# Retention value rows through DRAM and a broadcast DMA instead of broadcast products, on one core

## Chip, cores and metric

One Trainium2 chip, one core. The metric is the device time of one launch in microseconds (us); the kernel before takes 787.32 us, the median of 3 runs (786.14 to 787.53).

## The reference, cut to what matters

One layer of a hybrid decoder runs over 16 learned meta tokens, 256 prompt tokens and 8 samples of one token each, all in float32: RMSNorm, a mixer (gated convolution and retention), then a mixture of 16 experts. For the samples the retention carries a recurrent state of 4 heads x 256 x 512 per sample, which is read, changed and written back:

```
proj = h @ w_in          # glu_a, glu_b, q, k, v, g_ret, gate_a, gate_b
# per sample b and head h (one token, L = 1):
S_new[b,h] = gamma_h * S[b,h] + outer(k[b,h], v[b,h])   # 256 x 512
o[b,h]     = q[b,h] @ S_new[b,h]                        # 512
# prompt: the same with a decay mask over the tokens
x = x + W_o(sigmoid(gA) * Conv(h) + sigmoid(gB) * Retention(h))
x = x + HierMoE(RMSNorm(x))
```

32 states (8 samples x 4 heads) of 512 KB each go in and 32 come out.

## The kernel before, in words

The mixer is a list of 112 units (`UNITS`), each one block of 128 output features: 24 products over 8 blocks of depth in three parts (high times high, high times low, low times high). Units 0 to 15 are the convolution's gate, 16 to 31 q and k, 32 to 47 v, 48 to 63 g_ret, 64 to 79 the retention's output, 80 to 95 the gates, 96 to 103 the convolution's output, 104 to 111 w_o. All engines walk the same list in program order. For each unit ACT rounds a weight piece to its high part two units ahead (`hi`, L761), VectorE subtracts it for the low part (`lo`, L1101), TensorE multiplies (`passes`, L1602), and ACT or VectorE takes the result out of PSUM. SP loads weights, a chunk of 1 MB for two units, into 3 slots (`load_weights`, L594); its queue is in order.

For a v unit TensorE transposes the values back to tokens (L1700) and ACT copies them to `v_tok` (L891, L892); rows 16 to 23 of the third token tile belong to the samples. ACT and VectorE split those rows into a high and a low part in `v_two` (L963, L1265).

From unit `STEP0` = 37 on, each unit carries one of 22 retention steps k; `ON_AT`, which sets in which unit ACT and VectorE round the retention's parts, follows from it. Step k < 16 serves head k // 4 and two samples. What happens to a state n = 2k + j:

- POOL loads it into slot n % `SLOTS` (L654). There are 7 slots: four in `S_ring`, one in `S_five`, two in the idle `xT` (`S_more`).
- ACT multiplies it by gamma (`scaled`, L788): the odd one at the head of unit k, the even one at the end of the unit before.
- TensorE lays the sample's value row over all 128 partitions in a PSUM tile `vb` by a product of a one-column selector (`pick`, broadcast to 128 columns; made by ACT, L811 to L814) with `v_two` (L1762).
- VectorE adds k times that row to the state, in two halves (L1284), and frees the PSUM tile.
- POOL stores the state (L661) once VectorE has updated it; TensorE multiplies q with it one step later (`samp_o`, L1660), which counts `S_used`.

POOL's queue is written out by hand and in order: store(n), then wait that store(n - 1) has landed and that TensorE has used state n - 1, then load(n - 1 + SLOTS). Steps with k % 4 == 0 also make the prompt's new state (L1713, copied by ACT, L905, stored by POOL, L672), scores (L1723) and transposes (L1731); k % 4 == 1 the prompt's outputs (L1747). Later steps take means and variances (L1776, L1783) and, in 20 and 21, turn the last convolution rows. PSUM tiles go round 7 banks in one fixed order (`TILES`).

The convolution is 248 steps on VectorE (L1144, L1148), handed out per unit by `QUOTA` (3, 2 or 4 per unit; 1 from unit STEP0 + 15 up to 63; 4 from 64). What is left is done at unit 85 (`LN_SUM`), ahead of the layer norm's sum (L1120). After the last store POOL reloads `xT` with the tokens (L688), which the w_o units add to.

Of the kernel before, what the change touches and what calls it, by code (L numbers as in the profile page):

```python
# [5 lines left out]
D = 1024  # L6
# [154 lines left out]
FIRST = {}  # L161
# [3 lines left out]
STEP0 = FIRST["v"] + 5  # L165
SLOTS = 7
# [54 lines left out]
def _tiles():  # L221
# [3 lines left out]
    for w in range(NMIX):  # L225
        u = UNITS[w]
        s, i = u
        if s == "ret":
            if i % 2:
                add((("m", w), "A"))  # L230
        elif s in ("q", "k", "v", "glu_b"):
            add((("m", w), "A"))
        elif s in ("gate_b", "glu_a", "cout", "wo"):
            add((("m", w), "D"))
        elif s in ("gate_a", "gret"):
            add((("m", w), "A"))
        if FIRST["v"] < w <= FIRST["v"] + 16:
            add((("vt", w - 1 - FIRST["v"]), "A"))
        if STEP0 <= w < STEP0 + STEPS:
            k = w - STEP0  # L240
            if 4 <= k <= 16 and k % 4 == 0:
                for dt in range(2):
                    add((("S", k // 4 - 1, dt), "A"))
            if k < 16 and k % 4 == 0:
                add((("score", k // 4), "D"))
                add((("kt", k // 4, 0), "A"))
                add((("kt", k // 4, 1), "K"))
            if k < 16 and k % 4 == 1:
                for et in range(4):
                    add((("o", k // 4, et), "A"))  # L250
            if k < 16:
                add((("vb", k, 0), "D"))
                add((("vb", k, 1), "D"))
            if k >= 5 and (k - 5) % 4 == 0 and k <= 17:
                add((("ot", (k - 5) // 4), "A"))
            if k >= 6 and (k - 6) % 4 == 0 and k <= 18:
                add((("gm", (k - 6) // 4), "D"))
            if k >= 7 and (k - 7) % 4 == 0 and k <= 19:
                add((("gv", (k - 7) // 4), "A"))
            if k in (20, 21):  # L260
                add((("ut", k - 20), "A"))
        if w == FIRST["wo"] + 4:
            for tt in range(3):
                add((("xk", 0, tt), "D"))
            add((("lg", 0), "D"))
        if w == LN_MEAN:
            add((("lm",), "D"))
        if w == LN_VAR:
            add((("lv",), "A"))
# [52 lines left out]
def build(nc, A, W, L, H2, YD, C, C2, O):  # L322
# [4 lines left out]
    with ctx:  # L327
# [23 lines left out]
        pick = sb("pick", [56, NSAMP], f32r)  # L351
# [89 lines left out]
        S_more = xT[:, :, :].rearrange("p k n -> p (k n)")[:, 0:4 * DV].rearrange("p (s a e) -> p s a e", s=2, a=2)  # L441
# [31 lines left out]
        pick_ready, two_clear, vhi_ready, vlo_ready = sem("pick_ready"), sem("two_clear"), sem("vhi_ready"), sem("vlo_ready")  # L473
# [27 lines left out]
        def state(n):  # L501

            i = n % SLOTS
            return S_ring[:, i] if i < 4 else S_five if i == 4 else S_more[:, i - 5]
# [84 lines left out]
        def _(sp):  # L589
# [4 lines left out]
            def load_weights(c):  # L594
# [9 lines left out]
                sp.dma_start(raw[raw_slot(c)][:, :], src).then_inc(raw_in[raw_slot(c)], 16)  # L604
            for c in range(NCM + RS + 2):
                load_weights(c)
# [38 lines left out]
        def _(pool):  # L645
# [10 lines left out]
            def store(n):  # L656
                h, b = n // 8, n % 8
                dst = O["ret_sample"][0, b, h].rearrange("(t p) e -> p t e", p=128)

                evacuated(pool, ("vb", n // 2, n % 2))  # L660
                pool.dma_start(dst, state(n)[:, :, :]).then_inc(S_stored[n % SLOTS], 16)  # L661
# [23 lines left out]
            for i in (5, 6):  # L685
                pool.wait_ge(S_stored[i], 16 * len(range(i, 32, SLOTS)))
            pool.wait_ge(S_used, 32)
# [56 lines left out]
        def _(act):  # L744
# [66 lines left out]
            act.activation(pick[:, :], ident[0:56, 64:72], ACT.Copy).then_inc(pick_ready, 1)  # L811
            act.wait_ge(pick_ready, 1)
            act.activation(pick[0:24, :], ident[0:24, 16:24], ACT.Copy).then_inc(pick_ready, 1)
            act.activation(pick[32:56, :], ident[32:56, 48:56], ACT.Copy).then_inc(pick_ready, 1)  # L814

            for w in range(NMIX):
# [137 lines left out]
                if STEP0 - 1 <= w < STEP0 + 15 and (w - STEP0 + 1) % 4 == 0:  # L954
# [4 lines left out]
                    if h >= 2:  # L959
                        seen(act, ("vb", 4 * h - 5, 1))  # L960
# [123 lines left out]
        def _(dve):  # L1084
# [88 lines left out]
            for w in range(NMIX):  # L1173
# [86 lines left out]
                if STEP0 <= w < STEP0 + STEPS:  # L1260
# [13 lines left out]
                    if k < 16:  # L1274

                        h = k // 4
                        for j in range(2):
                            smp = 2 * (k % 4) + j
                            dve.wait_ge(S_scaled, 2 * k + j + 1)
                            seen(dve, ("vb", k, j))  # L1280
                            for dt in range(2):
                                st = state(2 * k + j)[:, dt, :]
                                f = 2 * h + dt
                                ins = dve.scalar_tensor_tensor(out=st, in0=bank(("vb", k, j))[:, :],  # L1284
                                                               scalar=kT[:, f, TP + smp:TP + smp + 1], in1=st,
                                                               op0=ALU.mult, op1=ALU.add)
                            free(ins)
# [287 lines left out]
        def _(pe):  # L1575
# [73 lines left out]
            def samp_o(s):  # L1649
# [4 lines left out]
                for j in range(2):  # L1654
                    smp = 2 * (s % 4) + j
                    evacuated(pe, ("vb", s, j))
# [7 lines left out]
            for w in range(NMIX):  # L1664
# [37 lines left out]
                if STEP0 <= w < STEP0 + STEPS:  # L1702
# [48 lines left out]
                    if k == 0:  # L1751
                        pe.wait_ge(qm_ready, 1)
                        pe.wait_ge(pick_ready, 3)
                    if 1 <= k <= 16:
                        samp_o(k - 1)
                    if k < 16:
                        h = k // 4
                        for j in range(2):
                            smp = 2 * (k % 4) + j
                            b = opened(("vb", k, j))  # L1760
                            pe.wait_ge(vlo_ready, h + 1)
                            done(pe.matmul(b[:, :], pick[:, smp:smp + 1].broadcast_to([56, 128]), v_two[0:56, h % 2, :], start=True, stop=True))  # L1762
# [224 lines left out]
```

## Time and profile before

| | us |
|---|---|
| median of 3 runs | 787.32 (786.14 to 787.53) |
| the profiled execution: its span | 784.6 |
| TensorE busy | 762.0 (97%) |
| VectorE busy | 667.3 (85%) |
| ScalarE (ACT) busy | 513.9 (66%) |
| GpSimd (POOL) busy | 97.0 (12%) |

The trace gives one time for the profiled execution, its span from the first instruction to the end of the last, 784.6 us; the median of the runs lies 2.7 us above it. Busy time counts an engine's instructions, not its waits. The chain of waits is followed back from the last instruction and tells which work set the end. DMAs are issued by SP, POOL and ACT queues and run beside the engines; "to landing" is the time from issue until the data is there.

### The profile page before, as it was taken

Reading aid. Unit: us, or ns where it says so; the run is one execution under the profiler, and the core shown is the slowest. Engines: PE = TensorE matmul, PEld = TensorE weight load, DVE = VectorE, ACT = ScalarE, POOL = GpSimd, SP = SyncE. Lnnn points to the kernel's source line nnn. Section 1 sums busy time; section 2 is a strip of 40 time slices with the busy share of each in tenths; the row PEclk is TensorE's granted clock in tenths of the full one; section 3 lists DMA queues with packets and bytes.
Section 4 is the critical chain, followed back from the end, with each engine's and each line's share of the span. In section 5 each row is a group of like instructions: output and inputs, shape, how many; then the busy total and the mean of one; then the engine's idle time right before and its main releaser. Section 6 shows DMA issues by size and latency. Waiting matters only on the chain.

```text
span 784.6 us, 12128 instructions
## 1 busy us (share of the span) xinstructions
PE 762.0 (97%) x4747; PEld 655.3 (84%) x4747; DVE 667.3 (85%) x903; ACT 513.9 (66%) x641; POOL 97.0 (12%) x120
## 2 busy tenths in 40 slices
PE   8999999999999999999999998999999999999994
PEld 5999999777777699999889975888888888888873
DVE  5699999877878979899977677998889998999897
ACT  7433445775858675345496463878888888887863
POOL 0100001224333200000002001111121111110000
PEclk9999999999999999999999999999999999999998
DMA  9935446599899756455449554999999999999962
GB/s 343 358 133 193 165 168 236 178 330 324 316 326 300 270 185 223 148 176 169 153 165 356 218 215 145 348 365 368 378 367 372 346 381 356 362 374 355 362 261 85
DMA packets 39174, 213.28 MB, mean 272 GB/s; under 512 B 7381, under 2 KB 7637, under 8 KB 19244
## 3 DMA queue, kind: packets, MB, share of 16 engines
q1 hardware_dynamic: 23268, 165.39, 56.8%
q0 software_dynamic: 15408, 45.71, 16.6%
q10 hardware_dynamic: 432, 1.31, 0.4%
q8 instruction: 40, 0.66, 0.3%
q14 instruction: 26, 0.21, 0.1%
HBM read 193.45 MB, written 31.65 MB: 287 GB/s over the span
## 4 chain that ended last, share of the span: by engine, by line
PE 80%; DVE 12%; ACT 4%; DMA 2%; issue 2%; DVEq 0%; ACTq 0%
PE bank L1874 34%; PE bank L1602 30%; DVE w_lo L1101 3%; DVE conv L1148 3%; PE bank L1747 2%; PE bank L1660 2%; PE bank L1713 2%; PE bank L1864 2%; DMA raw<-weights 1%; PE bank L1762 1%; PE bank L1776 1%; PE bank L1783 1%; ACT w_hi L761 1%; PE bank L1904 1%; DMA con<-constants 1%
## 5 line engine op out<-in xcount | busy, mean ns | idle before, releaser
L1602 PE MATMUL bank<-h_hi,w_hi 128*128 128x264 f32 (+1 forms) x640 | 188.7, 295 | 3.6 <-DVE w_lo L1101 3.3
L1602 PE MATMUL bank<-h_lo,w_hi 128*128 128x264 f32 (+1 forms) x640 | 184.0, 287 | 0.0
L1602 PE MATMUL bank<-h_hi,w_lo 128*128 128x264 f32 (+1 forms) x640 | 183.9, 287 | 0.0
L1106 DVE TENSOR_TENSOR ring_lo<-raw,ring_hi 128x2048 fp32r<-128x2048 f32 x72 | 163.6, 2289 | 23.4 <-ACT ring_hi L768 23.4
L1101 DVE TENSOR_TENSOR w_lo<-raw,w_hi 128x1024 fp32r<-128x1024 f32 x112 | 136.9, 1223 | 28.6 <-ACT w_hi L761 28.0
L761 ACT ACTIVATE w_hi<-raw 128x1024 fp32r<-128x1024 f32 x112 | 118.0, 1053 | 55.8 <-PE bank L1602 52.4
L768 ACT ACTIVATE ring_hi<-raw 128x2048 fp32r<-128x2048 f32 x72 | 138.4, 1922 | 19.6 <-PE bank L1874 19.6
L1602 PEld LDWEIGHTS bank<-h_hi,w_hi 128*128 128x128 f32 x640 | 120.4, 188 | 9.5 <-DVE w_lo L1101 5.0
L1602 PEld LDWEIGHTS bank<-h_lo,w_hi 128*128 128x128 f32 x640 | 120.4, 188 | 0.5 <-issue 0.2
L1602 PEld LDWEIGHTS bank<-h_hi,w_lo 128*128 128x128 f32 x640 | 120.2, 188 | 0.0
L1148 DVE SCALAR_TENSOR_TENSOR conv<-u,vec,conv 128x256 f32<-128x256 f32 x240 | 102.0, 482 | 0.6
L1874 PE MATMUL bank<-ring_hi,x_hi 128*128 128x512 f32 x192 | 76.0, 396 | 0.7 <-DVE x_lo L1460 0.7
L1874 PE MATMUL bank<-ring_lo,x_hi 128*128 128x512 f32 x192 | 75.2, 392 | 0.0
L1874 PE MATMUL bank<-ring_hi,x_lo 128*128 128x512 f32 x192 | 74.8, 389 | 0.0
L1106 DVE TENSOR_TENSOR w_lo<-raw,w_hi 128x2048 fp32r<-128x2048 f32 x24 | 55.0, 2291 | 6.3 <-ACT w_hi L768 6.3
L768 ACT ACTIVATE w_hi<-raw 128x2048 fp32r<-128x2048 f32 x24 | 46.1, 1923 | 6.3 <-PE bank L1874 4.4
L1874 PEld LDWEIGHTS bank<-ring_hi,x_hi 128*128 128x128 f32 x192 | 36.0, 188 | 8.9 <-DVE x_lo L1460 1.5
L1874 PEld LDWEIGHTS bank<-ring_lo,x_hi 128*128 128x128 f32 x192 | 36.0, 188 | 8.1
L1874 PEld LDWEIGHTS bank<-ring_hi,x_lo 128*128 128x128 f32 x192 | 36.1, 188 | 7.6
L718 POOL DMA_INDIRECT y_rows<-Y,idx x14 | 21.3, 1520 | 161.4 <-ACT Y L1063 161.4
L1874 PE MATMUL bank<-ring_hi,aT_hi 128*128 128x512 f32 x96 | 37.6, 391 | 0.0
L1874 PE MATMUL bank<-ring_lo,aT_hi 128*128 128x512 f32 x96 | 37.5, 390 | 0.0
(297 smaller groups left out, 1481.1 us busy)
## 6 DMA issues: line engine op xcount, KB each, us to landing
raw<-weights SPq DMA_DIRECT2D x152, 1024.0 KB, 7.0
S_ring<-in_state_ret POOLq DMA_DIRECT2D x20, 512.0 KB, 6.7
out_ret_sample<-S_ring POOLq DMA_DIRECT2D x20, 512.0 KB, 5.8
xT<-in_state_ret POOLq DMA_DIRECT2D x8, 512.0 KB, 5.8
out_ret_sample<-xT POOLq DMA_DIRECT2D x8, 512.0 KB, 7.7
S_five<-in_state_ret POOLq DMA_DIRECT2D x4, 512.0 KB, 6.4
out_ret_sample<-S_five POOLq DMA_DIRECT2D x4, 512.0 KB, 8.8
out_ret_prompt<-S_out POOLq DMA_DIRECT2D x8, 256.0 KB, 4.0
```

The source lines that it names most:

```text
L718: pool.indirect_dma_start(YD, bass.IndirectOffsetOnAxis(ap=idx[:, NE + e:NE + e + 1], axis=0), Y[:, e % 2, :], None, bounds_check=2 * N - ...
L761: act.activation(part_view(w_hi, w), raw_view(w), ACT.Copy).then_inc(hi_ready, 1)
L768: act.activation(ring_view(ring_hi, k), raw[raw_slot(c)][:, :].rearrange("p (k n) -> p k n", k=4), ACT.Copy).then_inc(chunk_hi, 1)
L1101: dve.tensor_tensor(part_view(w_lo, w), raw_view(w), part_view(w_hi, w).bitcast(f32), ALU.subtract).then_inc(lo_ready, 1)
L1106: dve.tensor_tensor(ring_view(ring_lo, k), raw[raw_slot(NCM + k)][:, :].rearrange("p (k n) -> p k n", k=4), ring_view(ring_hi, k).bitcast( ...
L1148: dve.scalar_tensor_tensor(out=out, in0=src, scalar=w_t, in1=out, op0=ALU.mult, op1=ALU.add).then_inc(conv_step, 1)
L1602: ins = pe.matmul(out, a[:, k, cols], b[:, k0 + k, :], start=first and k == 0 and j == 0, stop=last and k == ks - 1 and j == 2)
L1660: ins = pe.matmul(o_samp[q:q + NSAMP, :], qm[:, 2 * h + dt, smp, :], state(2 * s + j)[:, dt, :], start=s % 4 == 0, stop=s % 4 == 3)
L1713: pe.matmul(b[:, :], k_tok[:, tt, dt * 128:(dt + 1) * 128], v_tok[h][:, tt, :], start=tt == 0, stop=False)
L1747: ins = pe.matmul(b[:, f0:TP], v_tok[h][0:nt, tt, e0:e0 + 128], P[0:nt, col + f0 - t0:col + TP - t0], start=tt == 0, stop=tt == 2)
L1864: ins = pe.transpose(b[:, f * 128:(f + 1) * 128], xg[:, e % 2, at_f:at_f + 128], ident)
L1874: ins = pe.matmul(out, a[:, kk, :], b[:, kk, :], start=first and kk == 0 and j == 0, stop=last and kk == 3 and j == 2)
```

## The change

The `vb` products and `pick` go. A new DRAM tensor `VS` (`v_rows`) takes each head's 8 value rows (16 KB), written by SP as soon as the head's values are in `v_tok`; SP waits for it to land. Then SP reads, for each of the 16 steps, the two samples' rows over all 128 partitions (512 KB per step) into `v_all`, which has two buffers and lies where slots 5 and 6 lay. The broadcast for step k waits until VectorE has done step k - 2 (`S_new`, which VectorE counts once per state). VectorE reads the row from SBUF. The slots fall from 7 to 5, and STEP0 moves from 37 to 39, and with it QUOTA and ON_AT. Stores and sample products wait on `S_new` now.

```diff
-STEP0 = FIRST["v"] + 5
-SLOTS = 7
+STEP0 = FIRST["v"] + 7
+SLOTS = 5
...
-            if k < 16:
-                add((("vb", k, 0), "D"))
-                add((("vb", k, 1), "D"))
...
-        S_more = xT[:, :, :].rearrange("p k n -> p (k n)")[:, 0:4 * DV].rearrange("p (s a e) -> p s a e", s=2, a=2)
+        v_all = xT[:, :, :].rearrange("p k n -> p (k n)")[:, 0:4 * DV].rearrange("p (s a e) -> p s a e", s=2, a=2)
...
-            return S_ring[:, i] if i < 4 else S_five if i == 4 else S_more[:, i - 5]
+            return S_ring[:, i] if i < 4 else S_five
...
+            rows = {"k": 0}
+
+            def value_rows(w):
+
+                while rows["k"] < 16 and STEP0 + rows["k"] - 2 <= w:
+                    k = rows["k"]
+                    h, smp = k // 4, 2 * (k % 4)
+                    if smp == 0:
+                        evacuated(sp, ("vt", 4 * h + 3))
+                        sp.dma_start(VS[h], v_tok[h][16:24, 2, :]).then_inc(v_out, 16)
+                        sp.wait_ge(v_out, 16 * (h + 1))
+                    if k >= 2:
+                        sp.wait_ge(S_new, 2 * k - 2)
+                    sp.dma_start(v_all[:, k % 2], VS[h, smp:smp + 2, :].rearrange("(o b) e -> o b e", o=1).broadcast_to([128, 2, DV])).then_inc(vb_in[k % 2], 16)
+                    rows["k"] += 1
+
             for c in range(NCM + RS + 2):
+                value_rows(2 * c - 7)
                 load_weights(c)
...
-                evacuated(pool, ("vb", n // 2, n % 2))
+                pool.wait_ge(S_new, n + 1)
                 pool.dma_start(dst, state(n)[:, :, :]).then_inc(S_stored[n % SLOTS], 16)
...
-            for i in (5, 6):
-                pool.wait_ge(S_stored[i], 16 * len(range(i, 32, SLOTS)))
-            pool.wait_ge(S_used, 32)
+            pool.wait_ge(S_new, 32)
             pool.dma_start(xT[:, :, :], L["tokens_t"]).then_inc(xT_in, 16)
...
-            act.activation(pick[:, :], ident[0:56, 64:72], ACT.Copy).then_inc(pick_ready, 1)
-            act.wait_ge(pick_ready, 1)
-            act.activation(pick[0:24, :], ident[0:24, 16:24], ACT.Copy).then_inc(pick_ready, 1)
-            act.activation(pick[32:56, :], ident[32:56, 48:56], ACT.Copy).then_inc(pick_ready, 1)
...
                             dve.wait_ge(S_scaled, 2 * k + j + 1)
-                            seen(dve, ("vb", k, j))
+                            if j == 0:
+                                dve.wait_ge(vb_in[k % 2], 16 * (k // 2 + 1))
                             for dt in range(2):
                                 st = state(2 * k + j)[:, dt, :]
                                 f = 2 * h + dt
-                                ins = dve.scalar_tensor_tensor(out=st, in0=bank(("vb", k, j))[:, :],
+                                ins = dve.scalar_tensor_tensor(out=st, in0=v_all[:, k % 2, j, :],
...
-                            free(ins)
+                            ins.then_inc(S_new, 1)
...
-                    evacuated(pe, ("vb", s, j))
+                    pe.wait_ge(S_new, 2 * s + j + 1)
...
-                    if k < 16:
-                        h = k // 4
-                        for j in range(2):
-                            smp = 2 * (k % 4) + j
-                            b = opened(("vb", k, j))
-                            pe.wait_ge(vlo_ready, h + 1)
-                            done(pe.matmul(b[:, :], pick[:, smp:smp + 1].broadcast_to([56, 128]), v_two[0:56, h % 2, :], start=True, stop=True))
```

## Rows read from the trace of the kernel before

**Rows 1.** The page: busy us (share) and instructions, and the chain by engine
```profile
PE 762.0 (97%) x4747; PEld 655.3 (84%) x4747; DVE 667.3 (85%) x903; ACT 513.9 (66%) x641; POOL 97.0 (12%) x120
PE 80%; DVE 12%; ACT 4%; DMA 2%; issue 2%; DVEq 0%; ACTq 0%
```

**Rows 2.** The chain in order of time, steps: start us, us, what
```profile
143.26 0.33 PE bank L1700 x3
...
148.17 0.97 PE bank L1660 x8
149.14 0.65 PE bank L1762 x2
149.80 3.29 PE bank L1602 x24
...
273.89 0.97 PE bank L1660 x8
```

**Rows 3.** Stretches: window us, length, busy of engines, clock, DMA share, GB/s
```profile
156.50:238.40 81.90, 81.90 (x507) 60.44 (x506) 63.53 (x108) 56.89 (x98) 29.35 (x43) 1.00 0.94 323
148.10:273.80 125.70, 125.70 (x779) 91.65 (x778) 101.29 (x170) 88.82 (x147) 43.19 (x62) 1.00 0.88 301
```

**Rows 4.** POOL's queue in time: start, us, instruction, idle before and releaser
```profile
156.47 0.71 POOL L654 DMA_DIRECT2D S_ring<-in_state_ret  x1 [2.95 <-DMA out_ret_sample<-S_ring]
...
170.84 0.71 POOL L654 DMA_DIRECT2D xT<-in_state_ret  x1 [2.03 <-DMA out_ret_sample<-xT]
...
238.39 0.72 POOL L654 DMA_DIRECT2D S_ring<-in_state_ret  x1 [1.65 <-DMA out_ret_sample<-S_ring]
```

**Rows 5.** Waits, 130 to 280 us: who waited for whom, us, times, longest
```profile
POOL S_ring L654 <- DMA out_ret_sample<-S_ring: 27.0, 11, 4.9
POOL xT L654 <- DMA out_ret_sample<-xT: 18.0, 6, 5.0
POOL S_ring L654 <- PE bank L1660: 15.6, 3, 6.1
POOL S_five L654 <- DMA out_ret_sample<-S_five: 10.1, 3, 4.0
...
ACT S_ring L788 <- DMA S_ring<-in_state_ret: 1.4, 1, 1.4
```

**Rows 6.** DMA issues, 139 to 275 us (last row: whole span): count, KB, landing
```profile
out_ret_sample<-S_ring POOLq DMA_DIRECT2D x20, 512.0 KB, 5.8
S_ring<-in_state_ret POOLq DMA_DIRECT2D x16, 512.0 KB, 6.2
raw<-weights SPq DMA_DIRECT2D x7, 1024.0 KB, 8.7
out_ret_sample<-xT POOLq DMA_DIRECT2D x8, 512.0 KB, 7.7
out_ret_sample<-S_five POOLq DMA_DIRECT2D x4, 512.0 KB, 8.8
...
out_conv_sample<-S_out POOLq DMA_DIRECT2D x1, 32.0 KB, 2.9
```

**Rows 7.** DMA view of the first 40 us, in slices of 1 us
```profile
GB/s 0 37 146 295 310 298 440 438 434 426 418 426 436 418 448 409 430 429 333 204 410 418 434 180 293 498 213 373 426 389 426 434 406 442 193 246 299 430 373 188
```

**Rows 8.** Single lines: state update, scaling, pick, and landings on S_ring
```profile
139.84 2.73 DVE L1284 SCALAR_TENSOR_TENSOR S_ring<-bank,kT,S_ring 128x512 f32<-128x512 f32 x4
...
174.13 1.06 ACT L788 ACTIVATE S_ring<-S_ring 128x1024 f32<-128x1024 f32 x1
...
L811 ACT ACTIVATE pick<-con x1: 195/195/195, 16.7 to 16.7; 56x8 fp32r<-56x8 f32 x1
...
DMA to landing us min/median/max: 3.4/6.4/16.9
```

**Rows 9.** The chain before the layer-norm sum: start us, us, what
```profile
374.35 0.86 DVE conv L1148 x3
...
377.41 0.89 DVE conv L1148 x3
```

More of the change, by code:

```diff
@@ L319, with build @@
     _last[SLOT[_w]] = _w
-def build(nc, A, W, L, H2, YD, C, C2, O):
+def build(nc, A, W, L, H2, YD, VS, C, C2, O):
     f32, f32r = mybir.dt.float32, mybir.dt.float32r
@@ L350, in build @@
         rs2 = sb("rs2", [128, 3])
-        pick = sb("pick", [56, NSAMP], f32r)
         wrg = sb("wrg", [128, KT, 20])
@@ L472, in build @@
         S_stored = [sem(f"S_stored{i}") for i in range(SLOTS)]
-        pick_ready, two_clear, vhi_ready, vlo_ready = sem("pick_ready"), sem("two_clear"), sem("vhi_ready"), sem("vlo_ready")
+        two_clear, vhi_ready, vlo_ready = sem("two_clear"), sem("vhi_ready"), sem("vlo_ready")
+        S_new, v_out = sem("S_new"), sem("v_out")
+        vb_in = [sem(f"vb_in{i}") for i in range(2)]
         Sp_stored = [sem(f"Sp_stored{i}") for i in range(2)]
@@ L959, in _ @@
                     if h >= 2:
-                        seen(act, ("vb", 4 * h - 5, 1))
                         act.wait_ge(vlo_ready, h - 1)
@@ L1752, in _ @@
                         pe.wait_ge(qm_ready, 1)
-                        pe.wait_ge(pick_ready, 3)
                     if 1 <= k <= 16:
                         samp_o(k - 1)
-                    if k < 16:
-                        h = k // 4
-                        for j in range(2):
-                            smp = 2 * (k % 4) + j
-                            b = opened(("vb", k, j))
-                            pe.wait_ge(vlo_ready, h + 1)
-                            done(pe.matmul(b[:, :], pick[:, smp:smp + 1].broadcast_to([56, 128]), v_two[0:56, h % 2, :], start=True, stop=True))
                     if k >= 5 and (k - 5) % 4 == 0 and k <= 17:
@@ L1983 @@
     YD = nc.dram_tensor("y_rows", (2 * N, D), _mybir.dt.float32).ap()
-    build(nc, A, W, L, H2, YD, C, C2, O)
+    VS = nc.dram_tensor("v_rows", (NH, NSAMP, DV), _mybir.dt.float32).ap()
+    build(nc, A, W, L, H2, YD, VS, C, C2, O)
     r = _run(nc, [arrays], core_ids=[0])
```

## The prediction

> **What bounds the kernel now.** First the busy shares and the chain of waits: TensorE is busy 97% of the span and carries 80% of the chain, VectorE 12%, DMA 2% [rows 1]. So time is gained or lost where TensorE's own sequence gets shorter, or where it starts to wait. Then the stretch the change touches, the 16 retention steps. In the chain, the samples' output products (L1660) run from 148.17 (the second step) to 273.89 (the one behind the last), 125.7 us in 15 steps, 8.38 us each, and the broadcast products (L1762) stand in TensorE's sequence at 0.65 us a pair [rows 2]. TensorE is busy 100% of this stretch at full granted clock [rows 3].
>
> Third, the engine that isn't on the chain: POOL's queue, which stores a state, waits for the store before it to land, then loads a state into that slot. Load 9 is issued at 156.47 and load 28 at 238.39 [rows 4]: 19 loads in 81.92 us, 4.31 us per state, 8.62 per step. That is slower than TensorE's 8.38. From 130 to 280 POOL waits 27.0 + 18.0 + 10.1 us for stores to land and only 15.6 for TensorE [rows 5]. Two states cost it about one store landing (5.8 to 8.8 us by slot, 6.7 weighted) and two issues (0.72 each): 8.1 us [rows 5, 6]. So this loop runs at its own limit already; what keeps it off the path is that it loads 7 states ahead and began 7 states ahead. Last, the traffic: 323 GB/s in those 82 us at a DMA share of 0.94 [rows 3]. The share isn't the capacity: in the first 40 us the slices from 6 to 18 us stand at 409 to 448 GB/s, about 430 [rows 7].
>
> **The change, part by part.** *Broadcast products out:* 32 matmuls, 16 pairs of 0.65 us on the chain [rows 2], -10.5 us if TensorE stays the bound: 8.38 - 0.66 = 7.7 us a step. With them go 32 PSUM tiles, and VectorE's waits for them, none of which stands on the chain. *pick:* three ACT copies of 0.2 us at 16.7 us [rows 8], under TensorE's first products: nothing; if that cover went, 0.6 us. *State update from SBUF instead of PSUM:* 0.66 us apart now ((2.73 - 0.74) / 3 [rows 8]); the nearest row reading SBUF, a convolution step of half the width, is 0.29 apart (0.86 for three [rows 9]). Between equal and a tenth less; VectorE is 80% busy in the stretch (101.3 of 125.7 [rows 3]) and TensorE needs a state only one step later: nothing.
>
> *Value rows out:* four stores of 16 KB, each waited for by SP. The nearest row, a 32 KB store, lands in 2.9 us [rows 6]. Behind the wait stand the broadcast of that step and the next weights; the weights land in 8.7 us and are wanted five units (over 17 us) later, so nothing there. The first broadcast is issued some 3 us after the copy of the fourth v tile in unit 36, lands about 6 us later (as state loads do, 6.2 [rows 6]), and is wanted in unit 39, three units of 3.3 + 0.3 us [rows 2] on: just in time; that is what the 2 units are for. Later broadcasts wait until step k-2 is updated and are wanted at step k: 16 us against 6 to 9. So the wait itself is free while the landing stays below two steps.
>
> *The bytes of the broadcasts:* this is the expensive part. No row shows such a DMA. Each writes 512 KB. A step moves two loads, two stores, half a 1 MB weight chunk and a quarter of two 256 KB prompt stores: 2.75 MB, in 8.62 us 319 GB/s, as the row says (323). After: 3.28 MB. What does the added 0.52 MB cost POOL's loop? Below: nothing, if it fits where the queues have a gap; a gain is excluded, since more traffic doesn't make a store land earlier. Above: in proportion to today's bytes, 0.524 / 0.323 = 1.62 us. Between: 1.22 us at 430 GB/s, and only where the engines would have moved something else, 323 / 430 = 75% of the time: 0.92 us. I take 0.92, because the loop leaves gaps, and a step's traffic is nearer to today's stretch than to a pure stream of loads: 9.54 us per step, 4.77 per state.
>
> *Seven slots to five:* POOL now loads state n+4 where it loaded n+6. The last load, 31, is issued in its iteration 27; load 9 was issued in iteration 3, at 156.47. The lead shrinks by two states, 8.6 us. At today's landings every load would come some microseconds behind the time ACT wants to scale it: load 12's place at 170.84 becomes load 10's, which with 6.2 us of landing is there at 177, while ACT scaled state 10 at 174.13 [rows 4, 8]. ACT works in order, so evacuations behind it wait too, and TensorE with them. POOL's loop becomes the pace.
>
> *Sum for the steps:* 156.47 + 24 x 4.77 = 271.0 for the issue of load 31; then landing 7.2 (6.2 plus one share of the added 0.92), scaling 1.05 and the update of both halves 1.41 (0.66 + 0.74) [rows 8]: 280.7, against 273.89 for the same product now [rows 2]: **+6.8 us**. The 10.5 us of removed products disappear in TensorE's waits.
>
> *Two units later:* two plain units go ahead of the steps and two fewer come behind; the heads of units are alike. Nothing. The reload of xT comes later by what the steps take longer and is wanted first by the w_o units, 50 units on. on_hi's eighth part moves by one unit; no chain piece there.
>
> *Quota:* units 52 and 53 do 4 convolution steps instead of 1, under the steps' DMA limit, so free there (on the path 6 x 0.29). The last six fall away just before the layer-norm sum, where VectorE holds the chain: three steps 0.86 to 0.89 us [rows 9], six 1.7 us: **-1.7 us** (bounds 0 and -3.4, twice that, since the pieces between them may shrink too).
>
> Sum: +6.8 - 1.7 = +5.1. On the profiled span 784.6 gives 789.7; the median of the runs, 787.3, lies 2.7 above the span, so 792.4.
>
> A rule against a middle value: the rows show 323 GB/s and a peak near 430. The Trainium skill, DMA: Bandwidth & Descriptors (Specifications), gives 435 GB/s for the fabric and about 358 for one core's share of its memory. At 358 the step would take 9.15 us (an estimate from that page): 156.5 + 109.8 + 9.7 = 276.0, with the quota +0.4, no measurable change.
>
> **The rivals.** *A, the broadcasts cost the loop nothing but the slots bind:* 156.47 + 24 x 4.31 + 6.2 + 1.05 + 1.41 = 268.6, -5.3, with the quota -7.0: 780.3. For it: gaps in the traffic, a queue of its own. Against it: every transfer in the stretch already lands in 6 to 9 us where 512 KB at 430 GB/s need 1.2.
>
> *B, faster, TensorE remains the bound:* if the DMA engines can do here what they did in the first 20 us, 3.28 MB take 7.6 us at 430 GB/s, just under TensorE's 7.7; then -10.5 - 1.7 = -12.2: 775.1. It decides at a state cadence of 3.86 us. Against it: POOL's loop, of two landings and issues, would have to get shorter by a tenth under 19% more bytes. By the same page's 435 GB/s a step's bytes would fit like this; the retention rows don't agree so far.
>
> *C, the broadcast itself is late:* if its landing passes two steps (the longest landing on S_ring is 16.9 us [rows 8]), VectorE's update stands in order ahead of w_lo, and TensorE stops each step. At 10.2 us a step (the upper bound, 1.62) 156.47 + 24 x 5.12 + 10 = 289.4: +15.5 - 0 = 802.8.
>
> *D, the change does nothing measurable:* a broadcast costs the loop a third of the upper bound, 0.55 us, a step is 9.17 us, and 156.47 + 110.0 + 9.5 = 276.0 is +2.1, the quota -1.7: 787.7. What the broadcast writes is 128 rows of 4 KB, the leading dimension 128, so it should spread like the state loads; were it confined to a few engines, that would be C.
>
> **How the numbers follow.** A measurement of this kernel tells changes over about 0.2%, 1.6 us. Forecast 0.48; A 0.15; B 0.13; C 0.10; D 0.14. Faster: A and B, 0.28. Slower: forecast and C, 0.58. The forecast's own range, at 0.62 to 1.4 us per broadcast, is 788.5 to 798. The range for 8 in 10 reaches down over A (with the quota's bound of -3.4, 778.6) and up to C; it leaves out B and the far end of C: 778 to 802.
>
> **What would show it.** Right: TensorE has idle time in the steps and the first to last sample product takes 130 to 136 us; ACT's scaling (L788) waits for state loads by tens of us in total where it waited 1.4 [rows 5]; POOL's loads about 4.8 us apart; traffic near 345 GB/s in the steps. Wrong: POOL's loads 4.3 or less apart, no waits of ACT, TensorE at 100%. Wrong in another way: VectorE's update waiting for the broadcasts' landing.

## The result, and the profile after

The changed kernel takes 800.54 us (median of 4 runs) against 787.42 for the kernel before beside it, ratio 1.017 (95% interval 1.0151 to 1.0189): 13.1 us slower. The forecast was 792.4, 5.1 slower: right in direction, within the range, but well under half of the size. The profiled execution has a span of 796.5 us. Ratios leave out executions that ran with one die in a slower state; among all that follow there is one, of 844.5 us, in after_again.

The page after: the busy shares, the chain of waits by engine and by line, and ACT's scaling (count and shape | busy, mean ns | idle before and what ended it):

```profile
PE 761.5 (96%) x4715; PEld 656.9 (82%) x4715; DVE 667.1 (84%) x903; ACT 511.6 (64%) x638; POOL 97.4 (12%) x120
PE 71%; DMA 13%; DVE 9%; ACT 3%; issue 2%; POOL 1%; DVEq 0%; ACTq 0%; POOLq 0%
PE bank L1875 33%; PE bank L1611 31%; DMA out_ret_sample<-S_ring 7%; DMA S_ring<-in_state_ret 5%; PE bank L1865 2%; DVE w_lo L1109 1%; DVE conv L1156 1%; DMA out_ret_sample<-S_five 1%; PE bank L1905 1%; DVE S_ring L1293 1%; DMA con<-constants 1%; PE bank L1756 1%; ACT S_ring L801 1%; PE bank L1628 1%; PE bank L1654 1%
L801 ACT ACTIVATE S_ring<-S_ring 128x1024 f32<-128x1024 f32 x26 | 27.4, 1054 | 36.6 <-DMA S_ring<-in_state_ret 36.4
```

DMA holds 13% of the chain where it held 2% [rows 1]: stores of states 8% and loads of states 5%. TensorE's 32 products are gone (4747 to 4715 instructions), yet its busy time hardly falls (762.0 to 761.5), of which more at the end. ACT, which waited 1.4 us for state loads [rows 5], waits 36.4 us on S_ring alone.

The stretch from the second to the last sample product, and stretches of 10 us within it (columns as in [rows 3]):

```profile
153.39:292.75 139.36, 125.52 (x743) 92.56 (x742) 98.90 (x169) 85.68 (x141) 43.56 (x63) 0.94 0.91 333
```

```profile
170.00:180.00 10.00, 6.91 (x37) 3.96 (x36) 3.52 (x8) 3.32 (x6) 2.18 (x4) 0.94 0.97 374
180.00:190.00 10.00, 10.00 (x49) 9.16 (x47) 8.32 (x17) 9.63 (x18) 3.51 (x5) 0.72 0.94 288
190.00:200.00 10.00, 10.00 (x73) 7.68 (x72) 6.46 (x12) 4.49 (x12) 3.98 (x6) 1.00 1.03 402
230.00:240.00 10.00, 9.31 (x46) 7.72 (x47) 7.22 (x14) 6.38 (x14) 3.37 (x6) 0.66 1.00 388
270.00:280.00 10.00, 8.95 (x57) 6.10 (x55) 6.87 (x12) 3.49 (x6) 3.96 (x6) 1.00 1.02 419
```

It takes 139.4 us where it took 125.7 [rows 3], and TensorE, 100% busy before, is idle 13.8 us of it. The traffic rises from 301 to 333 GB/s on average. The granted clock, 1.00 before, is 0.94 on average.

POOL's queue after, its third and last load of the loop (start, us):

```profile
163.48 0.71 POOL L669 DMA_DIRECT2D S_ring<-in_state_ret  x1 [3.28 <-DMA out_ret_sample<-S_ring]
...
282.08 0.72 POOL L669 DMA_DIRECT2D S_ring<-in_state_ret  x1 [3.12 <-DMA out_ret_sample<-S_ring]
```

These are loads 7 and 31, 24 apart: 118.6 us, 4.94 per state, where the forecast had 4.77 and the kernel before has 4.31 [rows 4]. The landings in the steps (from 139 to 300 us: count, KB, median us) are longer than in [rows 6]: the stores on `S_ring` by 1.9 us, the loads by 1.3, the weights, which go out on SP's queue beside the broadcasts, by 0.9:

```profile
out_ret_sample<-S_ring POOLq DMA_DIRECT2D x26, 512.0 KB, 7.7
S_ring<-in_state_ret POOLq DMA_DIRECT2D x22, 512.0 KB, 7.5
raw<-weights SPq DMA_DIRECT2D x9, 1024.0 KB, 9.6
xT<-v_rows SPq DMA_DIRECT2D x14, 512.0 KB, 6.5
```

The waits from 130 to 300 us:

```profile
POOL S_ring L669 <- DMA out_ret_sample<-S_ring: 52.8, 18, 6.9
ACT S_ring L801 <- DMA S_ring<-in_state_ret: 36.4, 13, 6.4
DVE w_lo L1109 <- ACT w_hi L774: 27.6, 12, 6.5
POOL S_five L669 <- DMA out_ret_sample<-S_five: 20.3, 5, 6.9
DVE S_ring L1293 <- ACT S_ring L801: 11.5, 5, 4.1
```

POOL waits for stores (73.1 us on the two rings, 55.1 before [rows 5]), ACT for loads, and behind ACT, in its order, come the weight pieces that VectorE and then TensorE need: VectorE waits 27.6 us for them, 9.2 before. No row shows VectorE waiting for the broadcasts: they arrive in time. What is left to cost are their bytes, and the slots they took; the experiments tell these apart.

### The profile page after: what moved, and what is told of

Read it like the earlier page. It is cut to its first block, busy times and chain, and to the rows that moved or that the text cites. A ratio compares the mean times of both kernels' runs of the same rounds, so it can differ in the third digit from the quotient of the medians.

```text
span 796.5 us, 12031 instructions
## 1 busy us (share of the span) xinstructions
PE 761.5 (96%) x4715; PEld 656.9 (82%) x4715; DVE 667.1 (84%) x903; ACT 511.6 (64%) x638; POOL 97.4 (12%) x120
## 4 chain that ended last, share of the span: by engine, by line
PE 71%; DMA 13%; DVE 9%; ACT 3%; issue 2%; POOL 1%; DVEq 0%; ACTq 0%; POOLq 0%
PE bank L1875 33%; PE bank L1611 31%; DMA out_ret_sample<-S_ring 7%; DMA S_ring<-in_state_ret 5%; PE bank L1865 2%; DVE w_lo L1109 1%; DVE conv L1156 1%; DMA out_ret_sample<-S_five 1%; PE bank L1905 1%; DVE S_ring L1293 1%; DMA con<-constants 1%; PE bank L1756 1%; ACT S_ring L801 1%; PE bank L1628 1%; PE bank L1654 1%
## 5 line engine op out<-in xcount | busy, mean ns | idle before, releaser
L1611 PE MATMUL bank<-h_hi,w_hi 128*128 128x264 f32 (+1 forms) x640 | 191.4, 299 | 7.8 <-ACT con L866 3.3
L1611 PE MATMUL bank<-h_lo,w_hi 128*128 128x264 f32 (+1 forms) x640 | 186.5, 291 | 0.0
L1611 PE MATMUL bank<-h_hi,w_lo 128*128 128x264 f32 (+1 forms) x640 | 186.5, 291 | 0.0
L1611 PEld LDWEIGHTS bank<-h_hi,w_hi 128*128 128x128 f32 x640 | 122.7, 192 | 16.0 <-issue 9.9
L1611 PEld LDWEIGHTS bank<-h_lo,w_hi 128*128 128x128 f32 x640 | 122.7, 192 | 0.6 <-issue 0.2
L1611 PEld LDWEIGHTS bank<-h_hi,w_lo 128*128 128x128 f32 x640 | 122.5, 191 | 0.0
L801 ACT ACTIVATE S_ring<-S_ring 128x1024 f32<-128x1024 f32 x26 | 27.4, 1054 | 36.6 <-DMA S_ring<-in_state_ret 36.4
L1293 DVE SCALAR_TENSOR_TENSOR S_ring<-xT,kT,S_ring 128x512 f32<-128x512 f32 x52 | 36.0, 743 | 11.5 <-ACT S_ring L801 11.5
```

The source lines that it names most:

```text
L801: act.activation(v, v, ACT.Copy, scale=GAMMA[n // 8]).then_inc(S_scaled, 1)
L1293: ins = dve.scalar_tensor_tensor(out=st, in0=v_all[:, k % 2, j, :], scalar=kT[:, f, TP + smp:TP + smp + 1], in1=st, op0=ALU.mult, op1=ALU.add)
L1611: ins = pe.matmul(out, a[:, k, cols], b[:, k0 + k, :], start=first and k == 0 and j == 0, stop=last and k == ks - 1 and j == 2)
```

## The experiments

Two theories went in. **P** (pace): the state traffic that POOL's queue carries sets the pace, through the in-order wait for a store's landing, and the broadcasts' bytes lengthen the landings. **S** (slots): the two lost slots explain most of it. Later the rivals were a limit by bytes alone (C), by a state's round through its slot (R), and by TensorE (T). Times are medians; a ratio is to the kernel before on the same chip, with its 95% interval.

**Slots alone, slots5.** On the kernel before:

```diff
-SLOTS = 7
+SLOTS = 5
```

> The kernel before with 5 slots instead of 7 and nothing else changed (broadcast products kept, no broadcast DMAs, steps from unit 37). Theory P (pace: POOL's loop sets the pace, two states per store landing and two issues, and the broadcasts' bytes lengthen the landings): the loop keeps its 4.31 us per state, so load 31 goes out at about 260 us and the last sample product at about 270 to 276, as before (273.9); time 786 to 792. Theory S (slots: the lost lead of two states is most of the 13 us): 797 to 801, with ACT waiting for state loads by 20 us or more.

Measured 790.96, ratio 1.0056 (1.0039 to 1.0072), +3.8 us. P's range; S falls for this kernel. Load 31 goes out at 262.02, where P said about 260, and the loop's pace is (262.02 - 156.31) / 24 = 4.40. But the slots aren't free even here, though TensorE's products still cover much.

**Bytes away, no_bytes.** On the changed kernel:

```diff
-                    sp.dma_start(v_all[:, k % 2], ...)
+                    if k < 2:
+                        sp.dma_start(v_all[:, k % 2], ...)
```

> The changed kernel with only the first two of the 16 broadcast DMAs; from step 2 on VectorE reads the rows already there, so the samples' states are computed with wrong value rows (SP's waits, 5 slots, steps from unit 39, no products all stay). Theory P: POOL's loads come back to about 4.3 us apart, the stretch from the second to the last sample product shrinks from 139 to about 123 us, time 783 to 787. Theory S: the time stays at 796 to 801, since the slots are still 5.

Measured 787.55 (10 runs, 785.4 to 791.8), ratio 1.0004 (0.9987 to 1.0022), at the upper end of P's 783 to 787 and far from S's range. The bytes of 14 broadcasts cost 13.0 us, 0.93 each. But with products and bytes both away this kernel is only level with the one before: the 10.5 us have gone somewhere. The profiled execution was the slowest of its ten, 791.77 us; its loads are 4.52 apart.

**Bytes twice, bytes_twice.** SP waits for each broadcast and issues it again; VectorE waits for both.

```diff
+                    sp.dma_start(v_all[:, k % 2], ...)
+                    sp.wait_ge(vb_in[k % 2], 16 * (2 * (k // 2) + 1))
                     sp.dma_start(v_all[:, k % 2], ...)
```

> The changed kernel with every broadcast issued a second time after the first has landed: 16 more DMAs of 512 KB. Theory P: each costs the loop again what the first did, 1.26 us per step (2 x (4.94 - 4.31)), in 12 to 14 steps 15 to 18 us: 814 to 820; the loads 5.5 to 5.6 us apart. Theory S: the bytes matter little, 801 to 806.

Measured 823.41, ratio 1.0458 (1.0427 to 1.0489): +22.9 us over the changed kernel, more than either theory. The loads are (298.15 - 165.94) / 24 = 5.51 apart, as P said; what goes beyond P comes with a wait that the changed kernel lacks, for two landings in a row (130 to 320 us):

```profile
DVE S_ring L1295 <- DMA xT<-v_rows: 43.7, 12, 7.3
DVE S_five L1295 <- DMA xT<-v_rows: 11.0, 3, 4.7
```

So this is the mechanism of rival C of the prediction made real: rows that come too late stop VectorE. The changed kernel does not have it.

**The in-order wait loosened, lag2.** On the changed kernel, in POOL's loop:

```diff
-                if n >= 1 and n - 1 + SLOTS < 32:
-                    pool.wait_ge(S_stored[(n - 1) % SLOTS], ...)
-                    pool.wait_ge(S_used, n)
-                    load(n - 1 + SLOTS)
+                if n >= 2 and n - 2 + SLOTS < 32:
+                    pool.wait_ge(S_stored[(n - 2) % SLOTS], ...)
+                    pool.wait_ge(S_used, n - 1)
+                    load(n - 2 + SLOTS)
```

> The changed kernel, but POOL in iteration n waits for store n-2 instead of store n-1 to land and then loads state n+3 instead of n+4. Theory P (the in-order wait for a landing is the limit, not the DMA engines): more stores in flight, loads 4.0 to 4.4 us apart, traffic in the steps over 360 GB/s, time 780 to 790. Theory C (the DMA engines are full at the 320 to 350 GB/s seen): traffic and time stay, 797 to 803, and landings only grow longer.

Measured 805.78, ratio 1.0245 (1.0228 to 1.0262): 5.2 us slower, not 10 to 20 faster; C's 797 to 803 is missed too, though traffic and landings do as C said (328 GB/s over the steps, loads landing in 8.6 us). The waits of POOL, 130 to 320 us:

```profile
POOL out_ret_sample L676 <- DVE S_ring L1293: 103.5, 19, 29.0
POOL S_ring L669 <- DMA out_ret_sample<-S_ring: 9.2, 5, 3.5
```

POOL hardly waits for landings any more, it waits for VectorE, which waits for the loads; loads stay (283.18 - 162.18) / 24 = 5.04 apart. So at 5 slots the in-order wait can go without a gain. The run doesn't show that this wait was no limit, since it changes two things: POOL loads state n+3 instead of n+4, and with that shorter lead it is the state itself that isn't ready. The 5.2 us are about one pace of lead; that they come from it is likely, not shown.

**TensorE's work put back, products_back.** The changed kernel with the 32 products restored, results unused:

```diff
+                            b = opened(("vb", k, j))
+                            done(pe.matmul(b[:, :], pick[...], v_two[...], start=True, stop=True))
...
+                            seen(dve, ("vb", k, j))
```

> The changed kernel with the 32 broadcast products and their PSUM tiles put back on TensorE, their results unused (VectorE still reads the DMA's rows). Theory P (POOL's loop of stores and loads sets the pace of the steps, TensorE waits in it): the 10.5 us of products fit into TensorE's waits, 799 to 803. Rival T (TensorE's own sequence still sets the pace between the waits): 808 to 811.

Measured 804.16, ratio 1.0236 (1.0189 to 1.0284), between P's 799 to 803 and T's 808 to 811: +3.6 us over 800.54, of 10.5. About two thirds of the removed products lie in waits, more if set against after_again below. T, that TensorE's own sequence sets the pace of the changed kernel, doesn't fit.

**A sixth slot with the same bytes, slots6.** One broadcast of 256 KB per state, one step ahead:

```diff
-SLOTS = 5
+SLOTS = 6
...
+                    for j in range(2):
+                        if k >= 1:
+                            sp.wait_ge(S_new, 2 * k + j - 1)
+                        sp.dma_start(v_all[:, j], VS[h, smp + j:smp + j + 1, :].broadcast_to([128, DV]))
```

> The changed kernel with each state's row broadcast in a DMA of its own (256 KB, two buffers of one row each, issued one step ahead instead of two), which leaves room for a sixth slot: the same bytes, SLOTS = 6. Ring theory R (a state's round of load landing, update and store landing over the number of slots is the limit): one more slot gives 4.9 us of lead once and a faster round, 786 to 795. Theory C (the bytes alone are the limit, whatever the slots): 798 to 802. A miss upwards would be broadcasts that land too late with one step of lead: VectorE's updates would wait for them.

Measured 795.76, ratio 1.0105 (1.0075 to 1.0136): -4.8 us. That is the predicted 4.9 us of one slot's lead, once; the loads are still 4.8 apart ((275.22 - 164.67) / 23), so R's faster round isn't there. The shorter lead of the broadcasts does show: VectorE waits 17.5 us for rows in this run (slots in `S_ring` 11.2, `S_five` 3.9, the sixth 2.4), so the slot alone may be worth more.

**What the products are worth, free_rows.** The changed kernel with 7 slots and no DMA for the rows:

```diff
-                                ins = dve.scalar_tensor_tensor(out=st, in0=v_all[:, k % 2, j, :],
+                                ins = dve.scalar_tensor_tensor(out=st, in0=v_tok[h][:, j, :],
```

> The changed kernel with 7 slots, no broadcast DMAs and no value rows stored: VectorE takes rows of the head's prompt values, which lie over all partitions already, so the samples' states are computed with wrong rows. It shows what the removed products are worth by themselves. Theory P: POOL's loads stay 4.2 to 4.3 us apart, since its queue waits in order for each store, and give 780 to 785. Rival T (TensorE alone binds): all of 10.5 to 12 us comes, 775 to 777.

Measured 776.90, ratio 0.9868 (0.9830 to 0.9905): -10.7 us. The time is in T's range, not in P's. The stretch from the second to the last sample product, then POOL's third and last load of the loop, the last load of the kernel before, and POOL's waits (130 to 300 us):

```profile
153.30:269.00 115.70, 115.23 (x744) 86.65 (x743) 99.51 (x169) 85.30 (x140) 42.49 (x61) 1.00 0.91 318
```

```profile
161.13 0.71 POOL L652 DMA_DIRECT2D S_ring<-in_state_ret  x1 [3.35 <-DMA out_ret_sample<-S_ring]
...
256.78 0.73 POOL L652 DMA_DIRECT2D S_ring<-in_state_ret  x1 [2.31 <-DMA out_ret_sample<-S_ring]
```

```profile
253.08 0.73 POOL L654 DMA_DIRECT2D S_ring<-in_state_ret  x1 [5.69 <-PE bank L1660]
```

```profile
POOL S_ring L652 <- DMA out_ret_sample<-S_ring: 40.3, 14, 6.1
POOL xT L652 <- DMA out_ret_sample<-xT: 16.8, 6, 5.4
POOL S_five L652 <- DMA out_ret_sample<-S_five: 8.2, 3, 6.0
```

TensorE is 100% busy again, at full clock, in 115.7 us where the kernel before needs 125.7: all the products come back as time. But the loop didn't get faster. With 7 slots the third load is number 9 and the last 31, 22 apart: (256.78 - 161.13) / 22 = 4.35 per state, 8.7 per step, where TensorE now takes 7.7 and where the kernel before had 4.31, or 4.39 up to load 31. POOL waits 65.3 us for stores to land (55.1 before). So P was right about the loop and wrong about the time: a loop slower than TensorE doesn't show in the time while its lead lasts. How much of it is left can be read: the kernel before issues load 31 20.8 us ahead of the products of its step (253.08, 273.89), free_rows 12.2 us ahead (256.78, 269.00), and there ACT already waits 7.9 us for loads. The faster TensorE has used up what the old one left over.

**The same with the looser wait, free_rows_lag2.** The edits of free_rows and lag2 together.

> As the kernel before it in this list (7 slots, no broadcasts, rows of the prompt's values), but POOL waits for store n-2 and loads state n+5. If the in-order wait holds the loop, this frees it: loads under 4.1 us apart and 774 to 778. If the slots' round or the bytes hold it, nothing is gained over free_rows.

Measured 775.03, ratio 0.9847 (0.9818 to 0.9877): 1.9 us under free_rows, where the intervals overlap. The loads are (251.39 - 156.80) / 23 = 4.11 apart (numbers 8 to 31) and POOL waits 6.3 us for stores instead of 65.3. So here, with 7 slots and no broadcast bytes, the in-order wait was what held the loop at 4.35; the time hardly moves because TensorE fills the steps.

**The bytes with seven slots, seven_bytes.** As free_rows, but the broadcasts are issued and waited for, to DRAM:

```diff
+                    sp.dma_start(SC[k % 2], VS[h, smp:smp + 2, :]....broadcast_to([128, 2, DV]))
```

> The changed kernel with 7 slots again: the value rows are still stored, and the 16 broadcast DMAs still read them 128 times each, but write 512 KB to DRAM aside instead of to SBUF (there is no room for them beside 7 slots); VectorE waits for them but takes rows of the head's prompt values, so the samples' states are computed with wrong rows. Ring theory R (with 7 slots the same bytes are hidden, the lost slots are the root): 776 to 784. Theory C (3.28 MB a step are too much for the DMA engines in 7.7 us, whatever the slots): 788 to 796, loads 4.6 us or more apart.

Measured 791.27, ratio 1.0053 (1.0036 to 1.0070), 14.4 us over free_rows. C's range, R falls: 7 slots don't hide the bytes. The loads are (272.99 - 164.90) / 22 = 4.91 apart, as with 5 slots. The stretch of it:

```profile
154.04:285.07 131.03, 120.66 (x743) 88.59 (x742) 98.89 (x169) 84.01 (x138) 42.38 (x61) 0.99 0.96 345
```

The bytes went to DRAM here, not to SBUF, so this number stands a little apart.

**Six slots without bytes, slots6_free.** free_rows with `SLOTS = 6`.

> The kernel of free_rows (no products, no broadcasts, wrong rows from the head's prompt values) with 6 slots instead of 7. It stands between 776.9 (7 slots) and 787.6 (5 slots). Theory R (the wait comes when a state's round no longer fits into the slots' time at TensorE's 7.7 us per step: 7 x 3.86 = 27 us fits, 5 x 3.86 = 19.3 does not): 777 to 781, nearly all of the cost falling on the step from 6 to 5. If the lead alone counts, each slot costs its 4 to 5 us: 781 to 784.

Measured 781.75, ratio 0.9938 (0.9919 to 0.9957): 4.9 over free_rows, 5.8 under no_bytes. The lead alone, as the second case said, and not R's jump at the fifth slot. The loads are (260.21 - 161.62) / 23 = 4.29 apart. no_bytes keeps a little that these two lack (the stores of the rows, SP's waits, the first two broadcasts), so the 5.8 isn't a slot alone.

**The form of the broadcast, plain.** 512 KB of `state_ret` loaded instead of the broadcast.

> The changed kernel, but each of the 16 broadcast DMAs is replaced by a plain load of a 512 KB state from DRAM into the same buffer (no 4 KB row read 128 times); the samples' states are computed with wrong rows. If the broadcast's form costs nothing beside its bytes: 799 to 802, landing 6.5 us. If reading one row 128 times is slow or fast, the time moves by more than 3 us.

Measured 798.20, ratio 1.0138 (1.0113 to 1.0163), landing 6.8 us against 6.5. Rows of 4 KB read 128 times each cost what a plain load of the same size does, within 2.3 us and the noise.

**The changed kernel with the old steps, steps37,** and **a second measurement of the changed kernel, after_again.**

> The changed kernel with the retention steps back at unit 37 (STEP0 = FIRST v + 5), 5 slots and broadcasts as changed. My forecast took the move of 2 units as free but for the convolution quota: 800 to 804. Rival: the broadcasts then come too late for the first step of each head (row store 2.9 us, broadcast 6.5 us, one unit), VectorE waits for the rows and the time is 804 to 812.

> The changed kernel as it is, as the yardstick for the three beside it: 798 to 802.

steps37 took 797.91, ratio 1.0134 (1.0111 to 1.0158); after_again 803.12, ratio 1.0204 (1.0183 to 1.0224). The changed kernel itself thus came out 2.6 us apart in two measurements. Under the broadcasts, starting 2 units later costs 2.8 to 5.5 us by the ratios, the smaller within the intervals. From unit 37 the rows come late only a few times: VectorE waits 6.7 us for them in all,

```profile
DVE S_ring L1293 <- DMA xT<-v_rows: 5.2, 2, 2.7
```

and the kernel is still no slower; neither forecast nor rival said so.

**The quota and the move by themselves, quota_old, steps39, steps39_quota, steps40.** quota_old is the changed kernel, the other three the kernel before:

```diff
-STEP0 = FIRST["v"] + 5
+STEP0 = FIRST["v"] + 7          # steps39; + 8 in steps40
...
-QUOTA = [..., (STEP0 + 15, 1), ...]
+QUOTA = [..., (STEP0 + 13, 1), ...]     # quota_old, steps39_quota
```

> The changed kernel with the convolution quota's drop to 1 per unit at unit 52, where it was before, instead of at unit 54. My forecast gave the later drop -1.7 us, so this should be 1 to 2 us slower than the kernel after beside it, 801 to 803. Rival: the six convolution steps in units 52 and 53 delay VectorE's state updates there, and this is no slower or faster.

> The kernel before with the steps from unit 39 instead of 37 and nothing else (7 slots, products, no broadcasts). My forecast: the quota's -1.7 us and no more, 785 to 787. If starting the steps 2 units later costs by itself, as the 797.9 of steps37 against 800.5 suggests: 788 to 791.

> The kernel before with the steps from unit 39, but with the convolution quota's drop to 1 left at unit 52. The move alone gave 784.25 (2.8 us faster than before). If the quota is what gives it, as forecast: 786 to 788, no gain left. If the units' move gives it: 784 to 785.

> The kernel before with the steps, and the quota with them, from unit 40: three units later, the latest that the order of the g_ret units allows. If the gain is convolution steps taken from the stretch ahead of the layer-norm sum, and VectorE no longer holds the chain there after two units: 784 to 785, as steps39. If each unit gives another 1 to 1.4 us: 782 to 783.5.

quota_old took 803.64, ratio 1.0228 (1.0192 to 1.0263), no different from after_again. steps39 took 784.25, ratio 0.9961 (0.9948 to 0.9975); steps39_quota 786.78, ratio 0.9998 (0.9987 to 1.0008); steps40 784.92, ratio 0.9975 (0.9964 to 0.9987). So on the kernel before the move gives 2.8 us, and nearly all of it is the quota's. The chain of waits ahead of the layer-norm sum shows it, first steps39, then steps39_quota (start, us, what):

```profile
309.44 70.33 PE bank L1602 x576
379.77 0.45 PE bank L1795 x2
```

```profile
309.36 46.89 PE bank L1602 x384
356.25 0.02 issue
356.27 1.07 ACT w_hi L761
357.34 0.02 issue
357.36 1.23 DVE w_lo L1101
358.59 1.59 DVE conv L1148 x4
```

With six convolution steps fewer there, the chain is TensorE's without a break up to the mean's product; with them, as before [rows 9], it goes over to VectorE at 356. steps39, a change of one number, is the fastest complete kernel here, with steps40 within its interval.

**The best of the broadcast's line, slots6_steps37.** The edits of slots6 and steps37 together.

> The changed kernel with six slots (a 256 KB broadcast per state, one step ahead) and the steps back at unit 37: the best version with DMA broadcasts that I can put together. If the slot's 4.8 us and the units' 2.6 us add up: 792 to 794, still over the kernel before, since the broadcasts' 13 us stand against 10.5 us of products. If the shorter lead of the first broadcast bites: 796 to 799.

Measured 797.82, ratio 1.0121 (1.0099 to 1.0143): no better than either edit alone. Its second case names the range, but its reason isn't shown: VectorE waits 16.8 us for rows, no more than in slots6.

## Why the prediction was right or wrong

The runs form a table of medians, in which the cost of slots and bytes can be read apart (all without the products, steps from 39). Its rows aren't wholly alike: with 7 and 6 slots and no bytes the rows aren't stored either, and slots6 issues its broadcasts later and in halves.

| slots | no broadcast bytes | with them |
|---|---|---|
| 7 | 776.9 | 791.3 (to DRAM) |
| 6 | 781.8 | 795.8 (in halves) |
| 5 | 787.6 | 800.5 |

A slot costs 4.5 to 5.8 us in either column, the bytes 13.0 to 14.4 in any row. Within that they simply add. The pace of POOL's loads fits both:

| slots | no broadcast bytes, us per state | with them |
|---|---|---|
| 7 | 4.35 (free_rows), 4.31 to 4.39 (before) | 4.91 |
| 6 | 4.29 | 4.81 |
| 5 | 4.40 (slots5), 4.52 (no_bytes) | 4.94 |

It goes by the bytes and hardly by the slots, and a slot's price is about one pace. So P and S each had a part: the bytes cost 13 us and, once the products are gone, the two slots up to 10.7.

- **Products out:** forecast -12.2 with the quota if TensorE stays the bound (rival B, 775.1); free_rows shows 776.9. The term was right, 1.8 us off.
- **Seven slots to five:** this is the step that failed. Rival A, the changed kernel without the bytes, stands at 780.3, 5.2 us over B. It is 787.55, 10.7 over free_rows: 5.5 us of the 8.1 by which the forecast missed. The premise, "this loop runs at its own limit already", held: 4.35 us per state under a TensorE that needs 3.86. What failed is how much of two states of lead is really lost. The sum charges 2 x 4.31 = 8.6 us and gets back 3.4: with 7 slots its own terms put the last product at 156.47 + 22 x 4.31 + 8.66 = 260.0, where TensorE without its broadcast products comes only at 273.89 - 10.5 = 263.4. The runs don't show that slack. The sum has 8.66 us from the issue of load 31 to its last update (landing, scaling, update). In free_rows it is 10.5, which leaves 1.8 us up to the products at 269.00, and ACT has waited for six loads before:

```profile
264.30 2.93 DVE L1279 SCALAR_TENSOR_TENSOR S_ring<-v,kT,S_ring 128x512 f32<-128x512 f32 x4
```

By the sum the first slot taken would then cost 4.31 - 3.4 = 0.9 us; it costs 4.9 (slots6_free). The remainder of the 5.5 us is open: the pace is 4.52 in no_bytes instead of 4.31, but that trace is of an execution 4.2 us slower than the median, and no_bytes has the rows' stores and SP's waits beside the lost slots.
- **The same sum against the changed kernel's own trace:** two plain units take 6.5 us (the second step's sample product moves from 148.1 to 154.6 in steps39). Less these, load 7 goes out 0.5 us later than the sum has it, 24 x (4.94 - 4.77) = 4.1 us are pace, and from load 31 to the last product it is 10.7 instead of 9.7. The product forecast for 280.7 comes at 286.2.
- **The bytes:** forecast minus A is 12.1 us; measured 13.0 (after less no_bytes). Nearly right. By the paces a broadcast costs the loop twice 0.4 to 0.6 us, so 0.8 to 1.2 a step, where the forecast took 0.92. That the middle of two ends, 0 and 1.62, came so near was in part luck: no row priced such a transfer. Rival B needed the stretch to run near 430 GB/s; its mean is 333, though single stretches of 10 us reach 402 and 419.
- **Whose wait:** right. ACT waits for loads by tens of us (36.4), TensorE has idle time, and VectorE doesn't wait for the broadcasts, all named beforehand. The sizes are off the way the time is: loads 4.94 apart, not 4.8; the stretch 139.4 us, not 130 to 136; and 333 GB/s, not 345.
- **The removed products disappear in waits:** mostly. products_back gives 3.6 of 10.5 us (1.0 if set against after_again).
- **TensorE's clock:** the prediction has no term for it. On the chain it costs some 3 us, as the last section shows; what it costs off the chain no run separates.
- **Two units later, quota:** for the kernel before right in kind and a little small (-1.7 forecast, -2.8 measured). For the changed kernel not seen: quota_old shows no loss beside after_again (803.64 and 803.12), and the move costs 2.8 to 5.5 us by steps37, where it was to cost nothing. Why is open. In steps37 the stretch of the steps is 2.4 us shorter (136.9), but its profiled execution took longer than that of the changed kernel (800.62 and 798.49), so the two traces don't tell.

What sets the pace of 4.9 under the broadcasts is only partly shown. Without their bytes and with 7 slots it is POOL's in-order wait for landings (free_rows_lag2). At 5 slots with the bytes that wait can't be tried alone (lag2). It isn't a slot's round (seven_bytes and slots6 leave the pace), nor a fixed rate of the DMA engines (10 us stretches reach 402 and 419 GB/s, the mean is 333). What is shown is that it grows by bytes and that lead is spent once per slot.

## What to carry to other kernels

Before an engine's work is moved to DMA, test what the work is worth with free data in its place, and what the room costs that the DMA's buffers take: here the products were worth 10.7 us, two slots of lead cost up to 10.7, and 7 MB more of traffic in a stretch that already ran at 300 GB/s cost 13.

A prefetch loop slower than the engine it feeds stays hidden only while its lead lasts. So before the engine is made faster or slots are taken away, read from the trace how far ahead the last load is issued, and compare it with what a late load really needs until its use, the engines' order included: here 10.5 us, where median landing, scaling and update add up to 8.7. And when a pace is taken from first and last load, count the loads between them: the same iteration loads another state when the number of slots changes.

A change of several parts can hide a good one: moving the steps by two units was worth 2.8 us on its own.

## What the runs showed of the hardware

The granted clock of TensorE falls after some of the changed kernel's waits. In the chain of the changed kernel around 179 us:

```profile
166.27 10.76 DMA S_ring<-in_state_ret
177.03 0.02 issue
177.05 0.03 ACT S_ring L801
177.08 0.94 issue
178.02 1.04 ACT w_hi L774
179.06 0.30 ACT con L866
179.36 0.14 issue
179.49 5.94 PE bank L1611 x24
185.43 0.49 PE bank L1709 x3
```

TensorE is busy 6.91 of the 10 us from 170 to 180; then the stretch from 180 has a mean clock of 0.72, between the full level (2.4 GHz) and the half (1.2 GHz), and the unit's 24 products take 5.94 us where they took 3.29 [rows 2]. That is 2.7 us more work behind a wait, some 3 with the pieces behind it, and these are the only ones of TensorE on the chain in the steps. Over the whole stretch TensorE is busy 125.5 us, where free_rows, with the same products, is busy 115.2. An estimate from the mean clock, (1 - 0.94) x 139.4 = 8.4 us, has most of the difference: that is why its busy time did not fall with its instructions. Most of it lies beside transfers that hold the chain. The Trainium skill (TensorE: Matmul & The Clock Gate, Part 1) has the clock fall to the half after an idle time and rise again once busy; these rows agree.

A state load of 512 KB took 10.76 us on that chain, where the median is 7.5. The traffic was 402 GB/s from 190 to 200 us and 419 from 270 to 280, loads and stores together, at DMA shares of 1.03 and 1.02, while other stretches show a share of 0.94 at 288: the share tells whether transfers are open, not how much more would fit. The Trainium skill (DMA: Bandwidth & Descriptors, Specifications) has about 358 GB/s as one core's share of the memory and 435 for the fabric: with one core running, the first is passed here and the second is not by any 10 us stretch; single slices of 1 us in [rows 7] stand above it, at up to 498.

Some kernels that wait for the traffic scatter more than one that TensorE paces: no_bytes from 785.4 to 791.8 in 10 runs and quota_old from 800.7 to 810.8 in 6, against 782.8 to 786.5 in 11 of steps39. seven_bytes and lag2, with 4 runs each, don't (2.5 and 2.4 us).
